# Squared-ReLU MLP in exact-product form: gate scaling of one token half on ScalarE, paired adds on VectorE, and joint work reordered in both layers

## The reference, cut to what matters

```
h   = rms_norm(x) * (1 + scale) + shift
x   = x + gate * (square(relu(h @ w_mlp1)) @ w_mlp2)     # 1024 -> 4096 -> 1024, fp32
```

## Time and profile before

| | |
|---|---|
| median of 3 executions | 1803.98 us (1803.07 to 1807.21) |
| profiled execution, its own time | 1804.19 us |
| its span | 1802.2 us |
| mean granted clock of TensorE | 0.983 of full speed |
| TensorE busy | 1681.4 us, 93% |
| VectorE busy | 1176.8 us, 65% |
| ScalarE busy | 823.4 us, 46% |
| GpSimd busy | 271.1 us, 15% |

### The profile page before, as it was taken

One profiled execution on the slowest core, in us unless ns is written; L12 is line 12 of the kernel. 1 busy time (PEld: TensorE's weight loads), 2 busy tenths in 40 slices (PEclk: granted clock), 3 DMA queues, 4 the chain that ended last, 5 costly groups with the idle time before them and its releaser, 6 DMA issues. The chain is left out here.

```text
span 1802.2 us, 28988 instructions
## 1 busy us (share of the span) xinstructions
PE 1681.4 (93%) x11814; PEld 1489.5 (83%) x11814; DVE 1176.8 (65%) x1676; ACT 823.4 (46%) x1244; POOL 271.1 (15%) x212
## 2 busy tenths in 40 slices
PE   6999999989898999999999989899898989999998
PEld 4778897768778999899999869769677778989897
DVE  5374737677348797886987965653767484747472
ACT  5433326646227534535435463232655283527161
POOL 0243632301200000000000023362311200000000
PEclk9999999999999999999999999999999999999999
DMA  9541112200346348258276023122300355546251
GB/s 384 167 155 56 51 48 91 86 1 2 139 149 270 132 175 315 95 207 317 70 283 241 23 101 131 71 84 99 135 2 1 117 195 226 202 149 249 102 187 47
DMA packets 45456, 250.27 MB, mean 139 GB/s; under 512 B 5998, under 2 KB 7452, under 8 KB 26652
## 3 DMA queue, kind: packets, MB, share of 16 engines
q1 hardware_dynamic: 43420, 245.49, 36.9%
q10 hardware_dynamic: 1920, 3.15, 0.5%
HBM read 218.73 MB, written 26.74 MB: 136 GB/s over the span
## 5 line engine op out<-in xcount | busy, mean ns | idle before, releaser
L880 POOL TENSOR_TENSOR w_lo<-raw,w_hi 128x512 fp32r<-128x512 f32 x124 | 176.2, 1453 | 959.5 <-ACT w_hi L1017 937.1
L3473 PE MATMUL ps<-op_hi,w_hi 128*128 128x384 f32 x880 | 301.2, 342 | 20.5 <-DVE xT L2636 9.5
L3473 PE MATMUL ps<-op_lo,w_hi 128*128 128x384 f32 x880 | 298.0, 339 | 0.0
L3473 PE MATMUL ps<-op_hi,w_lo 128*128 128x384 f32 x880 | 298.0, 339 | 0.0
L1534 ACT ACTIVATE w_hi<-raw 128x1024 fp32r<-128x1024 f32 x96 | 101.4, 1058 | 200.3 <-PE ps L3473 140.1
L3473 PEld LDWEIGHTS ps<-op_hi,w_hi 128*128 128x128 f32 x880 | 167.3, 190 | 28.5 <-issue 16.8
L3473 PEld LDWEIGHTS ps<-op_lo,w_hi 128*128 128x128 f32 x880 | 167.5, 190 | 0.0
L3473 PEld LDWEIGHTS ps<-op_hi,w_lo 128*128 128x128 f32 x880 | 167.2, 190 | 0.0
L1470 ACT ACTIVATE w_hi<-raw 128x1024 fp32r<-128x1024 f32 x80 | 82.3, 1053 | 143.7 <-PE ps L3436 123.7
L3144 PE MATMUL ps<-w_hi,h_hi 128*128 128x256 f32 x448 | 131.2, 293 | 0.0
L2590 DVE TENSOR_TENSOR w_lo<-raw,w_hi 128x1024 fp32r<-128x1024 f32 x96 | 116.0, 1218 | 20.2 <-ACT w_hi L1534 20.0
(11 more groups left out here) (406 smaller groups left out, 3947.6 us busy)
## 6 DMA issues: line engine op xcount, KB each, us to landing
raw<-w_big SPq DMA_DIRECT2D x96, 1024.0 KB, 6.2
raw_m<-w_modl SPq DMA_DIRECT2D x21, 1024.0 KB, 5.8
op_hi<-op_cache SPq DMA_DIRECT2D x21, 768.0 KB, 4.7
op_lo<-op_cache SPq DMA_DIRECT2D x21, 768.0 KB, 6.3
raw<-w_modl SPq DMA_DIRECT2D x14, 1024.0 KB, 4.9
op_hi<-op_cache SPq DMA_DIRECT2D x21, 512.0 KB, 4.0
op_lo<-op_cache SPq DMA_DIRECT2D x21, 512.0 KB, 5.6
first_mod<-w_modl SPq DMA_DIRECT2D x8, 1024.0 KB, 21.0
```

Of the source, the lines that this page charges most:

```text
L880: ins = nc.gpsimd.tensor_tensor(w_lo[r][:, ks, :], src[:, ks, :], w_hi[r][:, ks, :].bitcast(F32), ALU.subtract)
L3473: ins = mm(bank(base + g, 0, h), wide(w)[:, k, g * P:(g + 1) * P], ops[hl][:, k, 0:h], start=(p in FRESH and k == 0 and q == 0), stop=(k = ...
```

## The change

Four things change.

- In phases 9 to 12 of layer 0 (`SCALED`) ScalarE reads the sums from PSUM, multiplies them by the gates and writes them to a new tile `x_add` (a pair of feature tiles for each half, in memory that a dead tile held): four activations per half, eight per phase. VectorE then adds two feature tiles to `xT` in one `tensor_tensor` of 128x768, two per phase. TensorE waits for `x_scaled` ahead of phases 11 and 13, where it waited for `x_done`.
- In layer 0's first quarter the work of phases 1 to 5 stands in another order on ScalarE and VectorE, and in every quarter that of phases 8 and 9 (and 2).
- In layer 1's first quarter the work of phases 1 to 5 stands in another order on both, and in every quarter that of phase 6.
- `norm_mlp` makes the low part of the second weight block earlier, and in layer 1 the difference `s2_1` as well.

The instructions of SP and GpSimd keep their order. The core of the diff:

```diff
+SCALED = (9, 10, 11, 12)
+    x_add = place("x_add", RH, [2, 2, HALF])
# ScalarE, layer 1, mlp_quarter1
+                    if q == 0 and P_ == 1:
+                        high_w1(0, 3, 0)
+                        high_a1(3)
+                        past_sums1(1, 0)
+                        continue
...
+                    if P_ == 6:
+                        past_sums1(5, 1)
# ScalarE, layer 0, past_sums
+                    if P_ in SCALED:
+                        nh = {9: 1, 10: 0, 11: 1, 12: 0}[P_]
+                        act.wait_ge(sem("big_done"), big.at(2 * P_ + c_ + 1))
+                        act.wait_ge(sem("x_done"), xd.at(2 * (P_ - 7) + c_ - 1))
+                        sums_ = banks_of(P_, c_, h)
+                        for a in range(2):
+                            for c_i, t0, t1_ in x_spans(0, 1):
+                                ins = nc.scalar.activation(x_add[:, c_, a, t0 - h:t1_ - h], sums_[:, a, t0 - h:t1_ - h],
+                                                           ACT.Copy, scale=mt[:, 40 + 4 * nh + 2 * c_ + a, c_i:c_i + 1])
+                        ins.then_inc(sem("x_scaled"), 1)
+                        return
# ScalarE, layer 0, mlp_quarter
+                    if P_ == 9:
+                        high_a(10, n_t, first)
+                    if P_ - 1 in SCALED:
+                        past_sums(P_ - 1, 1)
...
-                    if 6 <= P_ < 13:
+                    if 6 <= P_ < 13 and P_ != 9:
# VectorE, norm_mlp
+                low_first()
...
+                        late_sums(0)
                         low_second()
+                late_sums(1)
# VectorE, layer 1, mlp_quarter1
                     elif P_ == 6:
                         hid_low1(4, 0)
                         hid_low1(4, 1)
+                        low_w1(q, 7, 0)
                         hid_low1(5, 0)
                         hid_low1(5, 1)
+                        low_w1(q, 7, 1)
# VectorE, layer 0, evict
+                        if th == 1:
+                            dve.wait_ge(sem("x_scaled"), xsc.at(2 * (P_ - 9) + c_ + 1))
+                            k = 4 * nh + 2 * c_
+                            v.tensor_tensor(xT[:, k:k + 2, h:n_t], xT[:, k:k + 2, h:n_t], x_add[:, c_],
+                                            ALU.add).then_inc(sem("x_done"), 1)
+                            return
# VectorE, layer 0, mlp_quarter
+                    if P_ == 1 and first:
+                        s2_s4(0, 0)
+                        low_a(l, n_t, 3, first)
+                        low_w(3, 0)
...
+                    elif P_ == 9:
+                        low_w(10, 0)
+                        low_a(l, n_t, 10, first)
+                        s2_s4(1, 1)
+                        low_w(10, 1)
+                        t_sum(l, n_t, 1, 3, first)
+                    elif P_ == 8:
+                        low_w(9, 0)
+                        evict(8, 0)
+                        low_a(l, n_t, 9, first)
+                        low_w(9, 1)
# TensorE, product
-                    elif P_ in (9, 11, 13):
-                        pe.wait_ge(sem("x_done"), xd.at({9: 2, 11: 6, 13: 8}[P_] + c_ + 1))
+                    elif P_ == 9:
+                        pe.wait_ge(sem("x_done"), xd.at(2 + c_ + 1))
+                    elif P_ in (11, 13):
+                        pe.wait_ge(sem("x_scaled"), xsc.at({11: 2, 13: 4}[P_] + c_ + 1))
```

More of the change, by code:

```diff
@@ L2347, in residual, with norm_mlp @@
                 v_.add()
-            sums, los, his, ophi, tsum, hsq, kept, xd, land = [Tally() for _ in range(9)]
+            sums, los, his, ophi, tsum, hsq, kept, xd, land, xsc = [Tally() for _ in range(10)]
             land.n = 16
-            def norm_mlp(l, n_t, first_sums, low_second):
+            def norm_mlp(l, n_t, first_sums, low_first, low_second, late_sums):
                 mt = modt[l][:].rearrange("p (m c) -> p m c", c=2)
@@ L2525, in mlp_quarter1 @@
                         s1_1(q, 1)
-                    elif P_ == 1:
+                    elif P_ == 1 and q > 0:
                         s2_1(q, 0)
@@ L2717, in mlp_quarter @@
                         add_sq(6, 1, 1)
-                    if not (first and P_ == 1):
+                    if P_ != 8 and not (first and P_ == 1):
                         evict(P_, 0)
@@ L2725, in mlp_quarter @@
                         s1(part, 0)
-                    elif p == 1:
+                    elif p == 1 and not (first and P_ == 1):
                         s2_s4(part, 0)
@@ L2776, in first_sums1 @@
                         s1_1(0, 1)
-                    norm_mlp(l, n_t, first_sums1, low_second1)
+                    norm_mlp(l, n_t, first_sums1, lambda: low_w1(0, 1, 0), low_second1, lambda c_: s2_1(0, c_))
                     t_sum1(1)
@@ L3458, in mlp_quarter1 @@
                     turn_x(KD - 1, done + KD)
-            wlo, oplo, hev, hsq, kept, xd = [Tally() for _ in range(6)]
+            wlo, oplo, hev, hsq, kept, xd, xsc = [Tally() for _ in range(7)]
             opl = [Tally() for _ in range(3)]
```

129 lines of the change are left out of this document (88 added, 41 removed).

## The result

The changed kernel takes 1779.76 us (median of 4; 1775.60 to 1785.67) against 1804.18 us (median of 4): ratio 0.9865, 95% interval 0.9837 to 0.9894. In a second comparison it took 1779.73 us (median of 4) against 1805.14, ratio 0.9851 (0.9825 to 0.9877). The forecast was 1780.

The account below looks back on a forecast made before the run. TensorE was taken as the bound, with 29.8 us of waits in the MLP to win: -7.9 - 6.7 - 7.3 + 2.2 - 4.7 = -24.4, from 1804.19 to 1779.8, said as 1780 us; range 1773 to 1793.

Parts of the forecast that it names:

- A: Layer 0, first quarter, phases 2 and 3: the 6.00 us wait nearly goes, and the half clock behind it; -7.9 us.
- B: Layer 0, joints of phases 8 and 9, four quarters: waits of about 2 us fall to 0.5 us each; -6.7 us.
- C: Layer 0, joints of phases 9 and 10: waits go, as does half clock behind two of the 2 us waits; -7.3 us.
- D: Layer 0, phases 10 and 11: TensorE waits for ScalarE's scaling; +2.2 us, between -1.2 and +10.2; VectorE's relief worth nothing by itself.
- rival 1: Layer 0: ScalarE's scaling pieces cost their upper bound, 2.0 us more per quarter, 1788 us; chance 0.10.
- E: Layer 1: waits at phase 6's end go in three quarters (-1.7), the first quarter's waits shrink (-3.0); -4.7 us.
- rival 3: Half clock follows the remaining waits (layer 0's last quarter 2.2 us, layer 1's 1.8), 1.7 us each: 1785 us; chance 0.05.
- VectorE as bound of phases 8 and 9: Layer 0: VectorE's holes don't line up, phases 8 to 10 gain half, some half clock stays: 1792 us; chance 0.08.
- no gain: Whole kernel: each wait is replaced by another, nothing is won: 1804 us; chance 0.02.
- ScalarE as bound: Layer 0, phases 9 to 12: ScalarE decides once a scaled half takes 2.5 us; 1811 us at 3.0; chance 0.03.

## Why the prediction was right

**A** was right in its mechanism and size. The joint of 2 and 3 has 0.22 us where 0.4 was said; the half clock went with the wait, and came back with it in the kernel whose first quarter was undone. By starts the joint has -5.8 and the half clock -2.6 (-5.6 and -2.8 in the sum), and the 0.5 us left for later joints are 0.6, all ahead of phase 4: -7.8. The rest of the stretch's -8.0 is no part of A. The 0.65 us more ahead of phase 2 stay in the kernel whose first quarter was undone (1.02 us there too): they are what `norm_mlp`'s earlier low weights had won ahead of phase 1 (0.57), and phase 0 was 0.3 shorter by scatter.

**B and C** came out at -13.9 for -14.0, by parts: joints of 8 and 9 -7.9, of 9 and 10 -4.2, phase 9's own halves -1.8 (3.3 us of half clock gone, 0.3 to 0.4 a quarter of wait for the second eviction half come). VectorE's queue in phases 8 and 9 of the second quarter, changed kernel, against the earlier trace rows:

```profile
742.53 1.14 DVE L2710 SCALAR_TENSOR_TENSOR xT<-ps,modall,xT 128x384 f32<-128x384 f32 x2
744.07 1.76 DVE L2672 TENSOR_TENSOR op_lo<-op_t,op_hi 128x1536 fp32r<-128x1536 f32 x1 [0.39 <-ACT op_hi L1582]
...
749.27 1.14 DVE L2710 SCALAR_TENSOR_TENSOR xT<-ps,modall,xT 128x384 f32<-128x384 f32 x2
750.32 1.22 DVE L2657 TENSOR_TENSOR w_lo<-w_sum,w_hi 128x1024 fp32r<-128x1024 f32 x1
751.46 1.75 DVE L2672 TENSOR_TENSOR op_lo<-t2b,op_hi 128x1536 fp32r<-128x1536 f32 x1
```
The eviction's first half stands in the hole, which shrank from 1.45 to 0.39; `op_lo` of phase 10 comes one `w_lo` behind the second half. Phase 8's move alone is worth 8 us (measured by undoing it).

**D** had the right chain and the right records, with its result too large: +2.2 for a joint that has +1.0. The pieces, ScalarE by form, and the paired addition on VectorE, against the earlier trace rows:

```profile
L1598 ACT ACTIVATE x_add<-ps,modall 128x256 f32<-128x256 f32 x64 | 31.5, 492 | 0.0
L1598 ACT ACTIVATE x_add<-ps,modall 128x128 f32<-128x128 f32 x64 | 24.3, 379 | 15.0 <-PE ps L3570 15.0
```

```profile
L2703 DVE TENSOR_TENSOR xT<-xT,x_add 128x768 f32<-128x768 f32 x32 | 29.8, 954 | 11.9 <-ACT x_add L1598 11.9
```
379 and 492 ns for the 384 and 489 taken from the middle of the bounds, 954 ns for 953. That the first two came so close is luck: the bounds were 332 to 429 and 376 to 591 ns, and no row spoke for their middle. The awaited chain on ScalarE, second quarter:

```profile
754.46 1.06 ACT L1558 ACTIVATE w_hi<-w_sum 128x1024 fp32r<-128x1024 f32 x1 [3.81 <-DVE w_sum L2719]
755.43 1.04 ACT L1558 ACTIVATE w_hi<-raw 128x1024 fp32r<-128x1024 f32 x1
756.37 2.58 ACT L1598 ACTIVATE x_add<-ps,modall 128x128 f32<-128x128 f32 x8
758.80 1.11 ACT L1558 ACTIVATE w_hi<-raw 128x1024 fp32r<-128x1024 f32 x1
759.75 1.53 ACT L1582 ACTIVATE op_hi<-op_t 128x1536 fp32r<-128x1536 f32 x1
761.12 1.10 ACT L1558 ACTIVATE w_hi<-raw 128x1024 fp32r<-128x1024 f32 x1
762.07 2.65 ACT L1598 ACTIVATE x_add<-ps,modall 128x128 f32<-128x128 f32 x8
```
The awaited half is the first four of the last row's eight. The records overlap by more than I took: eight pieces from 756.37 to the next instruction at 758.80 are 2.43 us, 1.21 a half and not 1.37. The two halves ahead so are 0.3 us shorter; the awaited one is not, as its last record counts in full (the four take 1.40 us to the last one's end). The chain takes 9.0 us and not 9.3, and TensorE starts 0.25 us less late than said: the bracket of 0.38 is 0.55 us of lost starts, where the sum had 0.8. So the records were forecast within 5 ns and the cost of a half came out 12% lower: in a train of small activations it is the distance of starts that counts. The sum has slips here too. Two times 384 and 489 less 0.1 each are 1.35 and not 1.37, and the upper end of 2.04 us has no overlap taken off, as the middle has; with it the end is 1.64, D's upper end +5.4 and not +10.2, and rival 1 costs 3 us and not 8. The failed step of D is a sentence, not the sum: the relief was priced at nothing because in the kernel before no wait hung on it. Once B and C take 4 us out of two phases, VectorE's 22 us of work without a hole is what TensorE would wait for; reordering alone has those 3.2 us in each quarter. The sum was right only because both halves of the change were in it.

**E** failed in one place. In the first quarter the seven phases gave -4.0 (-3.0 was said; 1.4 us of it are half clock behind the old wait of 3.27 us, which the sum had left out) and the three later joints -0.7, -0.9 and -0.7, but the joint behind the first quarter's phases, at which nothing was forecast, grew from 1.18 to 2.52 us: `hid_lo` of phase 1 had been moved behind both low weights of phase 6 and ahead of the eviction of phase 5. The kernel with the scaling alone shows what the sum had wrong. Its layer 1 is that of before, no half clock followed its 3.27 us wait, and it waits 2.58 us at this joint, where the kernel before waits 1.18; yet from the first phase's start to the first slot it takes 52.34 us, as the kernel before. What sets that time is the chain that ends with a `hid_lo` of VectorE, not the sum of TensorE's waits, and the changed kernel ends it 2.7 us sooner (49.64), not the 4.0 that its phases gained. In the first profile half clock followed the wait (a stretch behind 1478.01, and one in phases 8 and 9 of the second quarter for comparison; the clock is the number behind POOL's):

```profile
1478.00:1481.00 3.00, 2.99 (x7) 2.39 (x8) 1.92 (x2) 2.97 (x6) 0.00 (x0) 0.53 0.99 408
746.00:751.00 5.00, 4.91 (x29) 4.59 (x28) 4.97 (x6) 2.44 (x2) 0.00 (x0) 1.00 0.54 190
```
Filling VectorE's hole with those two `hid_lo` took 1.2 us back. At equal spacing layer 1 gained 3.7 us in this profile and would have gained 5.0 without that half clock: the -4.7 lies between. So a part of rival 3 did come true, 1.3 us behind a wait that it didn't name. Of the eight profiles with 2.5 to 2.6 us at this joint three have it; the last quarter's 1.76 us ahead of phase 11 was never followed by it.

**The rivals.** ScalarE's price at the upper end, VectorE as bound of phases 8 and 9, no gain, and ScalarE as bound are out by the rows above. The last was approached from its side: at twice the scaling, S = 2.4 us from start to start, the gain was gone (1804.4 against 1805.1), but only through the awaited chain and the half clock behind it; phases 10, 12 and 13 didn't wait for ScalarE. Its own condition, from 2.5 us on, no run reached.

**The signs and the number.** Two of the named signs failed. The first quarter's row behind phase 8 is 0.74 and not below 0.6, and the mean clock of the profile is 0.982 and not above 0.983, for the slower mixers. The waits ahead of phase 11 were to be about 0.8 and once 2.2, and are 0.26 to 0.38 and once 1.76. One of the signs of being wrong came, once: half clock behind a joint that didn't have it. That the median of 1779.76 stands 0.04 us from the forecast's 1779.8 is luck: D was 1.2 us off, E up to 1.0 and phase 10 gave 0.4 that no term had, and four runs of the kernel lie 10 us apart. What was right is the sizes of A, B and C.

## What to carry to other kernels

Read the idle time of the engine that bounds the kernel joint by joint, and count what the engine it waits for does between one hole and the next; a move into a visible hole could be priced here to a few tenths of a microsecond a joint. Don't add up the waits of one stretch as gains: look when the last piece of the awaited engine's queue ends, since a shorter wait can come back at the next joint. Before calling relief on a busy engine worthless, shorten the phases by what the other edits gain and look at its queue again: two edits that give 1 and 9 us alone gave 25 together. Behind a wait of 2 us reckon with half clock in one case of two, behind more than 3 us in most: 1.3 to 2.6 us more. Price a train of small instructions by the distance of their starts.
